# Convolution and pooling of a streaming encoder layer as banded products over 16 channels x 8 phases, in a block of their own

## The reference

```python
x = layer_norm(x, ln0_g, ln0_b)
h = x @ w_in                          # 1024 -> 384 value | 384 gate | 384 pool | 256 query
a = causal_depthwise_conv(val * sigmoid(gate), conv_w, conv_b)     # width 31
a = silu(layer_norm(a))
p = pool_mixer(pool_in)               # trailing means over 2/4/8/16 less the frame, linear, scale
m = memory_cross_attention(q, mem)    # 4 heads, 256 memory tokens
x = layer_norm(ALPHA * x + concat(a, p, m) @ w_out)
u = causal_depthwise_conv(x @ w_up, ffn_conv_w, ffn_conv_b)        # width 3, 2 x 2816
x = layer_norm(ALPHA * x + (silu(u_gate) * u_value) @ w_down)
```

## Time and profile before

| | |
|---|---|
| median of 3 runs | 2083.57 us (2080.91 to 2083.67) |
| the profiled execution | 2081.61 us |
| its span in the profile | 2079.8 us |
| TensorE products busy | 1915.2 us, 92% of the span |
| VectorE, ScalarE, GpSimd busy | 79%, 47%, 11% |
| granted TensorE clock, mean | 0.969 of full |

### The profile page before, as it was taken

The page is one execution under the profiler, slowest core; times in us unless marked ns, Lnnn a source line. Parts: engine busy times, 40 slices in busy tenths (PEclk is TensorE's granted clock), DMA queues, the critical chain, the costliest instruction groups (busy, mean ns, idle before and its releaser), DMA issues.

```text
span 2079.8 us, 26573 instructions
## 1 busy us (share of the span) xinstructions
PE 1915.2 (92%) x8584; PEld 1580.4 (76%) x8584; DVE 1637.7 (79%) x2241; ACT 984.5 (47%) x1681; POOL 218.6 (11%) x263
## 2 busy tenths in 40 slices
PE   3999999669999849999999999999999798999997
PEld 2887878558878638888888778888888686887786
DVE  7979877568898557888888788777778767656899
ACT  4264351555555345555555655555555434324231
POOL 1010100001122201222122001000000000000111
PEclk9999999789999969999999999999999899999999
DMA  6130210523443363334434524222214557547543
GB/s 247 67 114 27 81 41 1 195 91 110 144 151 116 131 239 112 134 139 141 141 123 149 202 102 142 83 89 91 81 71 142 186 203 267 190 170 263 183 162 121
DMA packets 135506, 282.96 MB, mean 136 GB/s; under 512 B 10512, under 2 KB 66960, under 8 KB 135440
## 3 DMA queue, kind: packets, MB, share of 16 engines
q1 hardware_dynamic: 135440, 282.13, 38.3%
HBM read 182.48 MB, written 99.61 MB: 136 GB/s over the span
## 4 chain that ended last, share of the span: by engine, by line
PE 54%; DMA 4%; DVE 3%; issue 1%; ACT 1%; SPq 0%; DVEq 0%; ACTq 0%
PE prod_ps L1671 54%; DVE mov_lo L1852 1%; DMA y_scratch<-up_and_out 1%; DMA mov_raw<-wdown_sums_scratch 1%; DMA mov_raw<-x_operands 1%; ACT mov_hi L1718 1%; DVE sta_lo L1848 0%; DMA mov_raw<-in_ln_b 0%; DVE up_and_out L1888 0%; DMA mov_raw<-in_w_down 0%; DVE up_and_out L1885 0%; DMA up_and_out<-x_scratch 0%; ACT sta_hi L1711 0%; ACT prod_ps L1725 0%; DVE sta_raw L1864 0%
## 5 line engine op out<-in xcount | busy, mean ns | idle before, releaser
L1671 PE MATMUL prod_ps<-mov_hi,sta_hi 128*128 128x512 f32 x1848 | 727.5, 394 | 41.0 <-ACT prod_ps L1725 25.6
L1671 PE MATMUL prod_ps<-mov_lo,sta_hi 128*128 128x512 f32 x1848 | 725.5, 393 | 0.0
L1671 PE MATMUL prod_ps<-mov_hi,sta_lo 128*128 128x512 f32 x1848 | 725.2, 392 | 0.0
L1671 PEld LDWEIGHTS prod_ps<-mov_hi,sta_hi 128*128 128x128 f32 x1848 | 351.1, 190 | 119.6 <-ACT prod_ps L1725 27.7
L1671 PEld LDWEIGHTS prod_ps<-mov_hi,sta_lo 128*128 128x128 f32 x1848 | 350.8, 190 | 73.9
L1671 PEld LDWEIGHTS prod_ps<-mov_lo,sta_hi 128*128 128x128 f32 x1848 | 351.0, 190 | 73.3
L1848 DVE TENSOR_TENSOR sta_lo<-sta_raw,sta_hi 128x512 fp32r<-128x512 f32 (+1 forms) x340 | 223.5, 672 | 66.7 <-ACT sta_hi L1711 64.0
L1711 ACT ACTIVATE sta_hi<-sta_raw 128x512 fp32r<-128x512 f32 (+1 forms) x340 | 198.3, 611 | 161.7 <-PE prod_ps L1671 120.6
L473 DVE SCALAR_TENSOR_TENSOR conv_pool<-glu,conv_w,conv_pool 128x512 f32<-128x512 f32 x240 | 160.1, 746 | 0.0
L294 PE MATMUL wb<-x0t_hi,win_hi 128*128 128x512 f32 x352 | 137.6, 391 | 4.8 <-DVE win_lo L528 4.8
L294 PE MATMUL wb<-x0t_hi,win_lo 128*128 128x512 f32 x352 | 137.4, 390 | 0.0
(11 more groups left out here) (241 smaller groups left out, 2788.4 us busy)
## 6 DMA issues: line engine op xcount, KB each, us to landing
sta_raw<-in_w_up SPq DMA_DIRECT2D x88, 512.0 KB, 4.2
hidden_scratch<-up_and_out SPq DMA_DIRECT2D x44, 512.0 KB, 2.6
y_scratch<-up_and_out SPq DMA_DIRECT2D x16, 1024.0 KB, 7.3
sta_raw<-hidden_scratch SPq DMA_DIRECT2D x32, 512.0 KB, 4.4
up_and_out<-y_scratch SPq DMA_DIRECT2D x16, 1024.0 KB, 4.9
x_operands<-x_operands_out SPq DMA_DIRECT2D x56, 256.0 KB, 3.8
mov_raw<-x_operands SPq DMA_DIRECT2D x14, 1024.0 KB, 7.0
mov_raw<-in_w_down SPq DMA_DIRECT2D x44, 256.0 KB, 4.5
```

Source lines behind the costliest of these rows:

```text
L1671: last = pe.matmul(psum, w, x, start=(start and k == 0 and i == 0), stop=(stop and k == m - 1 and i == 2), skip_group_check=True)
```

## The change

Tokens are ordered by phase: tile n holds tokens n%8, n%8+8, ... of one half of the sequence, so that 128 partitions can hold 16 channels x 8 phases, and a lag of 8 tokens is one column. `project_phase` replaces `input_phase`: it normalises, projects and gates only, with transposed operands double-buffered, w_in in ten pieces by columns, and the transposes of the next chunk between the product tiles. It stores gated values and pooling inputs to `cp_d`. The mixing block starts with 48 groups of 16 channels. A convolution group (24) is 5 lags x 3 products of a 128x128 band matrix with 256 columns; the bands come from the host (`lag_bands`). A pooling group (24) is 2 or 3 lags x 2 products with bands that GpSimd builds, and VectorE then fixes the first two columns (`pool_edge`). Keys, weights and the rest of the old preparation stand between the groups. Five of the eight w_out row tiles are split after chunk 0; four of them are loaded behind the groups, the last once the fourth is split. In the feed-forward block the edge of the width-3 convolution becomes two tiles wide and is filled by four small copies a block (`fill_edge`).

Input block (SP, TensorE, ScalarE, VectorE):

```diff
+            def load_x(n):
+                if n in (4, 5):
+                    sp.wait_ge(win_lo, len(pieces))
+                if n >= RING:
+                    sp.wait_ge(x0_stored[n % RING], 16 * (n // RING))
+                    sp.wait_ge(tp_ready, 2 * (n - RING) + 2)
+                rows = a["x"][(n // 8) * HALF:(n // 8 + 1) * HALF, :].rearrange("(q r) d -> r q d", r=PHASES)[n % 8]
+                sp.dma_start(x0[:, n % RING, :], rows).then_inc(x_loaded[n % RING], 16)
+            def load_w(i):
+                part, k0, k1, slot, dst = pieces[i]
+                if i >= 7:
+                    sp.wait_ge(win_lo, i - 2)
...
+            def store_gated(c, t):
+                sp.wait_ge(gated, c * CT + t + 1)
+                sp.dma_start(phases_of(c, t * P), vg[:, 0, t, :].rearrange("p (u q) -> p u q", u=TT)).then_inc(glu_stored[t], 16)
...
+            def turn(c, i):
+                u, b = i // 2, i % 2
+                n = c * TT + u
+                pe.wait_ge(x0_ready, n + 1)
+                if 2 * TT * c + i >= 2:
+                    pe.wait_ge(lo_done, 2 * TT * c + i - 1)
...
+            for c in range(NCH):
+                for n in range(JT):
+                    project(c, n)
+                    if c + 1 < NCH and 1 <= n <= 2 * TT:
+                        turn(c + 1, n - 1)
...
             for u in range(TT):
...
+                weights_hi(u)
+                split_hi(0, 2 * u)
+                split_hi(0, 2 * u + 1)
+            for i in range(4, 7):
+                weights_hi(i)
+            for c in range(NCH):
+                for n in range(JT):
+                    evacuate(c, n)
+                    if c == 0 and n == 1:
+                        for i in range(7, 10):
+                            weights_hi(i)
+                    if c + 1 < NCH and 1 <= n <= 2 * TT:
+                        split_hi(c + 1, n - 1)
...
+            def norms(c, u):
+                if c < NCH:
+                    layer_norm(c * TT + u)
+                    layer_norm_end(c * TT + u)
...
+            for c in range(NCH):
+                if c == 0:
+                    gate(0, 0)
+                    for i in range(7, 10):
+                        weights_lo(i)
+                    norms(1, 0)
+                    norms(1, 1)
+                else:
+                    norms(c + 1, 0)
+                    norms(c + 1, 1)
+                    gate(c, 0)
+                lows(c + 1, 0)
+                norms(c + 1, 2)
+                lows(c + 1, 1)
+                gate(c, 1)
+                norms(c + 1, 3)
+                lows(c + 1, 2, 3)
+                gate(c, 2)
+                lows(c + 1, 4, 5, 6, 7)
```

Mixing block, SP (`gx_*` channel inputs, 4 slots; `gt_*` taps, 3 slots; `g_res` results, 4 slots):

```diff
+                slot = wo_use[n]
+                earlier = wo_use[:n].count(slot)
+                if earlier:
+                    sp.wait_ge(wo_l, max(i for i in range(n) if wo_use[i] == slot) + 1)
...
+            def load_group(n):
+                if n >= 4:
+                    sp.wait_ge(gx_lo, n - 3)
+                if n >= 4 + CONV_GROUPS:
+                    sp.wait_ge(g_fix, n - 3 - CONV_GROUPS)
+                src = cp_d[n * GROUP:(n + 1) * GROUP, :].rearrange("c (r q) -> (c r) q", r=PHASES)
+                sp.dma_start(gx_raw[:, n % 4, :], src).then_inc(gx_in[n % 4], 16)
+            def load_taps(n):
+                if n >= CONV_GROUPS:
+                    return
+                if n >= 3:
+                    sp.wait_ge(gt_lo, n - 2)
+                sp.dma_start(gt_raw[:, n % 3, :], a["conv_bands"][n * P:(n + 1) * P, :]).then_inc(gt_in[n % 3], 16)
+            def store_group(n):
+                if n < CONV_GROUPS:
+                    sp.wait_ge(g_out, n + 1)
+                else:
+                    sp.wait_ge(g_fix, n - CONV_GROUPS + 1)
+                for h in range(2):
+                    dst = mix_d[h * D + n * GROUP:h * D + (n + 1) * GROUP, :].rearrange("c (r q) -> (c r) q", r=PHASES)
+                    sp.dma_start(dst, g_res[:, n % 4, h * P:(h + 1) * P]).then_inc(g_stored[n % 4], 16)
...
+            for n in range(NG):
+                if n + 4 < NG:
+                    load_group(n + 4)
+                load_taps(n + 3)
+                if n == 3:
+                    sp.dma_start(r_memT, a["memT"].rearrange("(k p) m -> p k m", p=P)).then_inc(land[0], 16)
+                if n == 6:
+                    sp.dma_start(r_wk, a["w_mk"].rearrange("(k p) m -> p k m", p=P)).then_inc(land[1], 16)
+                if n == 9:
+                    sp.dma_start(psc[:, :], a["pool_scale"]).then_inc(land[3], 16)
+                    load_pool_weights()
...
+                if n:
+                    store_group(n - 1)
+            store_group(NG - 1)
+            for s in g_stored:
+                sp.wait_ge(s, 16 * 2 * NG // 4)
+            sp.wait_ge(prep_lo, 2)
+            load_chunk(sp, 0, 0)
+            for n in range(4, KT - 1):
                 load_wo(n)
...
             load_chunk(sp, 1, 1)
+            load_wo(KT - 1)
```

Mixing block, TensorE and ScalarE:

```diff
+            def group(n):
+                pe.wait_ge(gx_lo, n + 1)
+                if n >= 4:
+                    pe.wait_ge(g_out, n - 3)
+                bank, slot = g_bank[n % 4], n % 4
+                if n < CONV_GROUPS:
+                    pe.wait_ge(gt_lo, n + 1)
+                    for s in range(LAGS):
+                        cols = slice(LEAD - s, LEAD - s + QS)
+                        for i, (w, x) in enumerate(exact_parts(gt_h[:, n % 3, s, :], gt_l[:, n % 3, s, :], gx_h[:, slot, cols], gx_l[:, slot, cols])):
+                            last = pe.matmul(bank, w, x, start=(s == 0 and i == 0), stop=(s == LAGS - 1 and i == 2))
...
+                    for s in range(lags):
+                        cols = slice(LEAD - s, LEAD - s + QS)
+                        for i, x in enumerate((gx_h, gx_l)):
+                            last = pe.matmul(bank, band_h[:, first + s, :], x[:, slot, cols], start=(s == 0 and i == 0), stop=(s == lags - 1 and i == 1))
+                last.then_inc(g_mm, 1)
...
+            for n in range(NG):
+                group(n)
+                if n == CONV_GROUPS:
+                    keys()
...
+            def group_hi(n):
+                act.wait_ge(gx_in[n % 4], 16 * (n // 4 + 1))
+                if n >= 4:
+                    act.wait_ge(g_mm, n - 3)
+                act.activation(gx_h[:, n % 4, LEAD:LEAD + QS], gx_raw[:, n % 4, :], ACT.Copy).then_inc(gx_hi, 1)
...
+                act.wait_ge(gt_in[n % 3], 16 * (n // 3 + 1))
+                if n >= 3:
+                    act.wait_ge(g_mm, n - 2)
+                act.activation(gt_h[:, n % 3, :, :].rearrange("p s j -> p (s j)"), gt_raw[:, n % 3, :], ACT.Copy).then_inc(gt_hi, 1)
+            def group_out(n):
+                act.wait_ge(g_mm, n + 1)
+                if n >= 4:
+                    act.wait_ge(g_stored[n % 4], 32 * (n // 4))
+                if n < CONV_GROUPS:
+                    ins = act.activation(g_res[:, n % 4, :], g_bank[n % 4], ACT.Identity, bias=cb[:, n:n + 1])
+                else:
+                    ins = act.activation(g_res[:, n % 4, :], g_bank[n % 4], ACT.Copy)
+                ins.then_inc(g_out, 1)
...
+            for n in range(NG):
+                group_out(n)
+                if n + 3 < NG:
+                    group_hi(n + 3)
+                    taps_hi(n + 3)
+                if n == 8:
+                    act.wait_ge(land[0], 16)
...
+            for n in range(CT, KT):
+                wout_hi(n)
             chunk(1, 1, 0, None)
```

VectorE: `group_lo(n + 3)` and, ahead of it, `pool_edge(n)` run in step n:

```diff
+            def group_lo(n):
+                dve.wait_ge(gx_hi, n + 1)
+                cols = slice(LEAD, LEAD + QS)
+                dve.tensor_tensor(gx_l[:, n % 4, cols], gx_raw[:, n % 4, :], gx_h[:, n % 4, cols].bitcast(F32), ALU.subtract).then_inc(gx_lo, 1)
+                if n < CONV_GROUPS:
+                    dve.wait_ge(gt_hi, n + 1)
+                    h, l = (x[:, n % 3, :, :].rearrange("p s j -> p (s j)") for x in (gt_h, gt_l))
+                    dve.tensor_tensor(l, gt_raw[:, n % 3, :], h.bitcast(F32), ALU.subtract).then_inc(gt_lo, 1)
+            def pool_edge(n):
+                i = (n - CONV_GROUPS) * GROUP // POOL_GROUP
+                x, y = gx_raw[:, n % 4, 0:2], g_res[:, n % 4, 0:2]
+                dve.wait_ge(g_out, n + 1)
+                if n > CONV_GROUPS:
+                    dve.wait_ge(g_fix, n - CONV_GROUPS)
+                link(dve.tensor_tensor(edge[:, :], y, x, ALU.add))
+                link(dve.tensor_tensor(edge[:, :], edge[:, :], ratio[:, 2 * i:2 * i + 2], ALU.mult))
+                dve.tensor_tensor(y, edge[:, :], x, ALU.subtract).then_inc(g_fix, 1)
```

ScalarE in the feed-forward block, and the host's bands:

```diff
+            def fill_edge(b, w):
+                if w == VALUE:
+                    act.wait_ge(c22, num(b) + 1)
+                    act.wait_ge(c21, num(b) + 1)
+                else:
+                    act.wait_ge(c12, num(b) + 1)
+                first = ub[:, w, 0:EDGE].rearrange("p (r t) -> p r t", t=P)
```

(72 more changed lines are left out.)

818 lines of the change are left out of this document (357 added, 461 removed).

## The result

The changed kernel takes 2110.49 us (median of 4 runs, 2108.40 to 2111.38) beside 2082.78 for the kernel before (2080.91 to 2083.67): ratio 1.0133, 95% interval 1.0115 to 1.0150. The forecast was 2110. The profiled execution has a span of 2109.4 us, 29.6 above the one before.

What follows compares the result with a forecast made beforehand. TensorE was taken to bound the input block, with load turns pacing the new groups. The terms -80+121+19.2-44.5+11+1 gave +27.5 us on the profiled 2081.6, forecast 2110; range 2082 to 2142, the forecast's own 2096 to 2130.

Steps and rivals of the forecast that it cites:

- What bounds the kernel: Input block: TensorE is the full engine, VectorE's convolution costs no time; the third channel tile's tap products on TensorE do.
- Part 1: Projection block alone: head 35, products 242 and 10.6, stall with half clock 16, tail 4.5; block change at 308, 80 less.
- Part 2: 48 groups ahead of the preparation: stretch of 121 us, bounds 93 and 157; first scores at 448.5 against 432.9.
- inserted work: Loads, small transfers and ScalarE's wide copies among the groups: 21 us in all, 12 taken as paid.
- the turn: Convolution groups: stores, load issue, landing, split and evacuation before buffers free, 5.5 us for three groups; 2.05 a group taken.
- Pooling: 24 pooling groups at 1.95 us each, paced by edge fix and load, 47 us, plus 4 for keys and wide copies.
- Part 3: Five w_out rows behind chunk 0: TensorE waits 8.5 us before chunk 1, plus 2.5 of half clock, +11 (6 to 13).
- Part 4: The rest: chunks unchanged, ScalarE's extra work in the up projection costs only at stage changes, +1 us (0 to 3).
- A: Rival: loads hidden in the groups, stretch 80 us, 41 less, 2069 in all; decides under 93 us; chance 0.23.
- B: Rival: TensorE at half clock in the convolution groups, 3.2 us a group, 25 more, 2135; chance 0.11.
- C: Rival: transfers queue, landings 5 (taps) and 3.5 us (groups), 2.5 a group of either kind, +36, 2146; chance 0.12.
- D: Rival: no stall in chunk 0 of the projection block, 2094 us; chance 0.06.

Runs made afterwards that it cites:

- Experiment 1: Changed kernel with the last three weight pieces split before the evacuation of tile 0 instead of behind that of tile 1; span 2102.2 us.
- Experiment 2: Experiment 1's kernel with the transposes of chunk 1 standing two product tiles later in chunk 0; span 2093.3 us.
- experiment 6: Changed kernel with only the two stores of each convolution group one group later in SP's queue; span 2107.8 us, groups 2 to 23 in 55.23.
- experiment 5: Changed kernel with six raw tap slots instead of three, tap loads two groups further ahead and stores one group later; span 2102.7 us, groups 2 to 23 in 46.65.
- experiment 7: Changed kernel loading two of five lags' taps from the fourth group on (128 KB, not 320; output wrong); span 2102.7 us, groups 2 to 23 in 54.18.
- Experiment 4: Changed kernel with VectorE copying away each pooling group's first two raw columns, so later loads skip waiting for the edge fix; span 2097.8 us.
- Experiment 3: Changed kernel with five w_out rows loaded during the pooling groups and split under the fold, instead of behind chunk 0's attention; span 2105.8 us.
- experiment 11: Changed kernel with the edits of experiments 2 to 5 together (five raw tap slots), plus one store for both halves of a group; median 2057.62 us, ratio 0.9881.

## Why the prediction was right

Point by point, by its own steps.

- **What bounds the kernel.** Right. VectorE's 240 convolution instructions are gone, and the first stretch is shorter by 80.4 us with the 85 us of tap products on TensorE, a head shorter by 7 and a stall that costs 16; these make 76 of it.
- **Part 1.** Head 33.5 for 35; stall 13.9 for 13.5 (its terms add up to 13.3); behind it products start 0.43 apart until 66.4 and 0.23 from then, about 2.2 us for the 2.5 taken; block change 307.9 for 308. Experiments 1 and 2 confirm the cause: with the load earlier and the transposes later the gap is gone.
- **Part 2.** Right in mechanism, 5 us short in size. Fill 13.9 for 15. Convolution groups: 59.5 us for 21, where the text had 43 and 12 of inserted work for both stretches. The term that was mis-sized is the turn, 5.5 us for three groups: a tap load lands in 5.0 here and not in 3.0, two stores take 0.9 of the queue and not 0.7, a group load's issue beside others 0.45 and not 0.35. With these it is about 7.7 as an estimate, or 2.6 a group, 54 for 21, and inserted work then has some 5. (The 7.5 in the expectation of experiment 6 comes out near it by luck: it takes 4.3 for the landing and adds the tap load's own issue, which a landing already holds.) Experiments 5, 6 and 7 each shorten that turn, and the time falls by 12.8, 4.2 and 5.3: enough to say that the turn was a limit. But 6 gave about 60% of what the sum of durations promised, and 7 less than 40% with the landing of this stretch. With the ring of experiment 5 the wait for taps goes and one for result slots comes. So the sum of the turn explains the direction and not the size. Two of the largest waits left in experiment 7 stand behind inserted transfers; what takes the rest isn't shown.
- **Pooling.** 52.9 with keys and copies, for 51. Two errors cancel here: a steady pace of 1.70 for 1.95 (a load in a quiet queue lands in 2.1, and I took 2.4), but 34.1 us from group 24 to 36, 2.8 each. That is 14 more than twelve groups at 1.70, though ScalarE's wide copies in it are only 5.5 us long and the text had a little over half of them paid. The rest is the copies' delay of fix and load, and 3.8 us of waiting for TensorE behind the key products. Experiment 4 takes the fix out of that loop; the same twelve groups then take 21.8, and the first scores come 15.7 earlier.
- **Part 3.** The gap ahead of chunk 1 is 8.65 us, for 8.5. The clock is at 0.59 over the next 4.7 us, and the two stages together lost 9.6, for 11. Experiment 3 removes it.
- **Part 4.** Nothing to be seen: 1328.6 for 1329.4 us.
- **Rivals.** A (loads hidden, 80 us) is what a better order of transfers comes nearer to in experiment 11: the stretch from block change to fold falls from 126 to 100 us, still above the bound of 93. It wasn't so in the change as made: ScalarE waited 57.6 us for loads. B (half clock in the convolution groups): the clock is 0.91 there and 0.96 in experiment 5, so the cost is small; the pooling groups run at 0.59, where TensorE has time to spare. C (transfers queue): its landings of 5 and 3.5 were nearer to those of the convolution groups, 5.0 and 4.3, than mine, and its 2.5 us for a convolution group is near the 2.6 estimated above; its 2.5 for a pooling group is not what the steady ones take (1.70). By its own terms C adds about 32 us and not 36, so 2142. D is refuted by the gap. So landings as long as C's were there in the convolution groups, where the forecast had shorter ones.

The forecast's end, 2110 for 2110.5, owes something to chance: its terms are off by +5 (groups), -3 (chunk 0), +1.5 (rest of the mixing block) and -2 us (feed-forward block). Inside the groups, too long a price for the steady pooling groups covers part of what the others cost more.

What stays open: why a gain at the first scores did not always reach the end. Of the 15.7 us in experiment 4, 11.6 did; chunk 0 took 1.7 us more (between 35.5 and 37.8 in runs that left it alone), the rest of the mixing block 0.5 and the feed-forward block 2.0 (between 1327.5 and 1330.9 with the same code). Open too are the part of the convolution groups that the turn doesn't explain, and the gain of the single store.

## What to carry to other kernels

When small transfers feed small pieces of work, follow the buffer back: which wait frees the slot, where the load stands in its queue, and which instruction of the consumer stands behind it in program order. Here no engine was full, and the time was set by two round trips through one queue, that of the taps and that of the pooling inputs. The change removed 85 us of products from a full TensorE and put 126 us of groups, half of them waiting, where 25 us of preparation had stood; with the slots free a few microseconds earlier, the operands of two stalls split earlier, one store for two and the same arithmetic, it is a gain of 1.2%. And inserted work can cost more than its own length where the loop around it passes through the engine that does it: here 5.5 us of copies stood in a stretch that was 14 us longer than its steady pace.

## What the runs showed of the hardware

- A DMA share of 0.88 wasn't a limit in the changed kernel. It moved 266 GB/s at 0.88; with a deeper ring 298 GB/s went at 0.92. The landing of a 128 KB load was 1.9 us at least, 2.1 in the median in the quiet pooling groups from 416 us on, and 4.3 in the convolution groups. The Trainium skill, "DMA: Bandwidth & Descriptors", section "Anatomy of one DMA", gives a fixed part of 2.0 us and 436 GB/s on top for GpSimd's path, 2.3 us for 128 KB as an estimate. The trace, with SP's queue, comes 0.2 under it for a load in a quiet queue (2.1), and it is 2 us over it where loads stand close; there the measured 4.3 decides.
- An issue on SP's queue took 0.32 to 0.35 us alone and 0.43 to 0.5 back to back, so load, taps and two stores take 1.9 to 2 us of the queue for each group, as long as TensorE's products (1.8).
